# Order of the state product, the y products and level 8 in the time mixer's scan

## The chip, the cores and the metric

The kernel runs on one core of one Trainium2 chip. The metric is the device time of one execution, in microseconds. Five engines of the core matter: TensorE (PE in the profile, its weight loads listed apart as PEld), VectorE (DVE), ScalarE (ACT), GpSimd (POOL) and SyncE (SP), which here issues all transfers. Each engine works through its own list of instructions in order; the lists meet only at semaphores. Everything is fp32.

## What is computed

The model has two layers over 1024 latent tokens and 256 context tokens of width 1024. Layer 0 mixes with a grouped Fourier transform, layer 1 with a bidirectional RWKV-7 time mixer. The change is in layer 1's recurrence. For each of 16 heads, with a state s of 64 x 64, and for both directions:

```python
def step(s, inp):
    r_t, w_t, k_t, v_t, a_t, b_t = inp
    sa = einsum('bhij,bhj->bhi', s, a_t)
    s = s * w_t[:, :, None, :] + sa[..., None] * b_t[:, :, None, :] + v_t[..., None] * k_t[:, :, None, :]
    return s, einsum('bhij,bhj->bhi', s, r_t)
```

The context tokens are run first, and only their final state is used; the latent tokens start from it and give y.

## The kernel before

The work ahead of the scan (layer 0, then the features of layer 1, written to scratch in DRAM) and behind it (normalisation, gate and output projection) is not touched by the change.

The scan (function `scan`) takes two heads at a time (h = 0, 1 on partitions 0 to 63 and 64 to 127), so there are 8 outer turns j. Each goes through 10 chunks of 128 tokens, of which the first two are context and the other eight latent. A chunk is done as two sub-chunks of 64 tokens, sub 0 and sub 1, in both directions d at once. Within a sub-chunk the recurrence is put in matrix form. That needs the inverse of a triangular 64 x 64 matrix per direction and sub-chunk, which is built by doubling: levels 2, 4, 8, 16 and 32. For level k TensorE makes a first product (`t`, masked by VectorE into TT with `copy_predicated`) and a second one (`m`, copied by ScalarE to M, which VectorE then transposes to MT for the next level's second product). The last product is copied as XT.

The scan is software-pipelined over chunks. In one period (function `period`, written out by hand on each engine) the chunk c goes through its sequential part (Q_ in the code), chunk c+1 through the second stage of the inverse, levels 4 to 32 (B_), chunk c+2 through the first stage, its operand products and levels 2 and 4 (A_), and chunk c+3 gets its operands from GpSimd. There is no planner: the order on each engine is the order of the calls in its `period`.

The sequential part of a sub-chunk is a chain across engines:

- `r` (TensorE, L1779): what the state Q contributes; ScalarE copies it to R (L1558).
- `sa` (TensorE, L1789): XT times R, into bank 7; ScalarE copies it to Z in two instructions, one per head (L1563). This is "SA's copy"; the semaphore is `asa`.
- `state` (TensorE, L1799): BKt times Z, into bank 6. VectorE adds the decayed old state SP of GpSimd (L1492) and writes the new Q (L1669), for which the next `r` waits.
- for latent chunks `y_state` (TensorE, L1809) and `y` (TensorE, L1814) accumulate the outputs in bank 7; ScalarE copies them to Y (L1569), and SyncE stores them.

All level products are issued from one helper (L1729) and go by their operands. Those of the second stage share bank 5: the `m8` product (MT, TT as operands), then `t16` (M, AT), which waits for ScalarE's copy of `m8`. ScalarE's `second` is L1554. The first stage's operand products are L1722, in two groups d = 0, 1; behind the second one ScalarE copies AT (`first_at`, L1542) and VectorE writes masked parts of ar (`first_ak`, L1636); ScalarE's `first_bk` (BKt, L1546) waits for the latter. VectorE's order after `first_ak` is: state addition, the transpose MT of level 8 (L1658), `first_x` (mask MT1, then transpose M, L1629), the mask of t16 (L1615), and so on.

In the weight loads' shapes, `r`, `state` and `y` use a stationary operand of 128 rows by 64 columns, `sa`, `y_state` and all level products one of 64 x 64, and the operand products one of 64 x 128. Each fp32 matmul of the code is two instructions in the trace: a level product of 8 matmuls is listed as x16, an `r` of 4 as x8.

Of the kernel before, what the change touches and what calls it, by code (L numbers as in the profile page):

```python
# [1328 lines left out]
def count(per, j, cc, i):  # L1329

    n = PER[per]
    full, rest = divmod(cc, NCH)
    return j * sum(n) + (full * sum(n) + sum(n[:rest]) + i)
# [8 lines left out]
def scan(nc, es, sem, ps, A, fe_d, v_d, y_d, w_last):  # L1342
# [35 lines left out]
    is_lat = lambda cc: cc % NCH >= 2  # L1378
# [5 lines left out]
    def ge(eng, s, v):  # L1384

        if v > 0:
            eng.wait_ge(s, v)

    def chunk_done(eng, j, cc):

        if is_lat(cc):
            ge(eng, py, count("y", j, cc, 2))
        else:
            ge(eng, pst, count("state", j, cc, 2))

    def turn(sub, t):

        return t[:, 0:4:3] if sub == 0 else t[:, 1:3]
# [5 lines left out]
    def gcol(rows, banks, c):  # L1404

        return ps[rows, banks, :].rearrange("p e (b c t) -> p e b c t", b=2, c=4)[:, :, :, c, :]
# [21 lines left out]
    with nc.Block() as block:  # L1428
# [98 lines left out]
        @block.scalar  # L1527
        def _(act):
            act.wait_ge(msk, NMSK)

            def exps(j, cc):
                s, l = par(cc), lng(cc)
                act.wait_ge(cum_ready, count("two", j, cc, 2))
                chunk_done(act, j, cc - SETS)
                act.activation(E1[l][:, 0:264].rearrange("p (b y) -> p b y", y=66)[:, :, 1:CK + 1], cum[s][:], ACT.Exp, scale=-DECAY).then_inc(exp_ready, 1)
                ge(act, op_ready, count("operands", j, cc - 2, 2))
                act.activation(E3[s][:], cum[s][:], ACT.Exp, scale=DECAY).then_inc(exp_ready, 1)  # L1537

            def first_at(j, cc):
                act.wait_ge(pa, count("first", j, cc, PA["g1"]))  # L1540
                for h in two:
                    act.activation(d4(AT[par(cc)][own(h)]), gcol(own(h), slice(2 * h, 2 * h + 2), 3 * h), ACT.Copy).then_inc(aa, 1)  # L1542

            def first_bk(j, cc):
                act.wait_ge(da, count("dve_first", j, cc, DA["ak1"]))
                act.activation(BKt[lng(cc)][:].rearrange("p h (d b) t -> p (h d) b t", b=2), gcol(slice(0, P), slice(0, 4), 2), ACT.Copy).then_inc(aa, 1)  # L1546

            def first_m2(j, cc):
                act.wait_ge(pa, count("first", j, cc, PA["m2"]))
                act.activation(M[par(cc)][:], lev(4), ACT.Copy).then_inc(aa, 1)  # L1550

            def second(j, cc, name):
                act.wait_ge(pb, count("second", j, cc, PB["mt32" if name == "xt" else name]))
                act.activation((XT if name == "xt" else M)[par(cc)][:], lev(5), ACT.Copy).then_inc(ab, 1)  # L1554

            def r(j, c, sub):
                act.wait_ge(pr, count("two", j, c, sub + 1))
                act.activation(Rs[sub][:], seq(6), ACT.Copy).then_inc(ard, 1)  # L1558

            def sa(j, c, sub):  # L1560
                act.wait_ge(psa, count("two", j, c, sub + 1))
                for h in two:
                    act.activation(turn(sub, Z[lng(c)][own(h), h]), seq(7)[own(h)], ACT.Copy).then_inc(asa, 1)  # L1563

            def y(j, c, sub):
                if sub == 0:
                    ge(act, y_st[par(c)], j * 256 + (c - 2) // 2 * 64)
                act.wait_ge(py, count("y", j, c, sub + 1))
                act.activation(turn(sub, Y[par(c)]), seq(7), ACT.Copy).then_inc(ay, 1)  # L1569

            def period(j, c, ahead):
                A_, B_, Q_ = c + 2 >= 0 and (ahead or c + 2 < NCH), c + 1 >= 0 and (ahead or c + 1 < NCH), c >= 0
                if B_:
                    second(j, c + 1, "m4")
                if Q_:
                    r(j, c, 0)
                if ahead or c + 3 < NCH:
                    exps(j, c + 3)
                if Q_:
                    sa(j, c, 0)  # L1580
                if A_:
                    first_at(j, c + 2)
                if B_:
                    second(j, c + 1, "m8")
                if A_:
                    first_bk(j, c + 2)
                if Q_ and is_lat(c):
                    y(j, c, 0)
                if Q_:
                    r(j, c, 1)  # L1590
                    sa(j, c, 1)
                if B_:
                    second(j, c + 1, "m16")
                if Q_ and is_lat(c):
                    y(j, c, 1)
                if A_:
                    first_m2(j, c + 2)
                if B_:
                    second(j, c + 1, "xt")

            for j in range(KT):
                for c in range(0 if j else -3, NCH):
                    period(j, c, j < KT - 1)
# [104 lines left out]
        def _(pe):  # L1708
# [50 lines left out]
            def m(j, cc, k):  # L1759
                s = par(cc)  # L1760
                pe.wait_ge(db, count("dve_second", j, cc, DB[f"t{k}"]))
                level(lev(5), MT[s], TT[k][s], pb)
# [6 lines left out]
            def at(sub, d):  # L1769
                return 2 * d + (sub if d == 0 else 1 - sub)  # L1770
# [20 lines left out]

            def state(j, c, sub):
                l = lng(c)
                if not is_lat(c):
                    pe.wait_ge(asa, count("four", j, c, 2 * sub + 2))
                if c == NCH - 1 and sub == 1:
                    return
                for d, h in pairs:
                    mm = pe.matmul(seq(6)[own(h), d, :], BKt[l][:, h, at(sub, d), :], Z[l][:, h, at(sub, d), :], start=True, stop=True)  # L1799
                mm.then_inc(pst, 1)  # L1800

            def y_state(j, c, sub):
                l = lng(c)
                pe.wait_ge(asa, count("four", j, c, 2 * sub + 2))
                if sub == 0:
                    pe.wait_ge(drm, count("rmask", j, c, 1))
                for d, h in pairs:
                    o = own(h)
                    pe.matmul(seq(7)[o, d, :], ar[l][o, at(sub, d), 1, :], Q[l][o, h, at(sub, d), :], start=d == 0, stop=False, skip_group_check=True)  # L1809

            def y(j, c, sub):
                l = lng(c)
                for d, h in pairs:
                    mm = pe.matmul(seq(7)[own(h), d, :], RBK[l][:, h, at(sub, d), :], Z[l][:, h, at(sub, d), :], start=False, stop=True, skip_group_check=True)  # L1814
                mm.then_inc(py, 1)

            def period(j, c, ahead):
                A_, B_, Q_ = c + 2 >= 0 and (ahead or c + 2 < NCH), c + 1 >= 0 and (ahead or c + 1 < NCH), c >= 0
                a, b = c + 2, c + 1
                lat = Q_ and is_lat(c)  # L1820
                if Q_:
                    r(j, c, 0)
                if B_:
                    m4(j, b)
                if A_:
                    products(j, a, 0)
                if B_:
                    t(j, b, 8)
                if Q_:
                    sa(j, c, 0)  # L1830
                if A_:
                    products(j, a, 1)
                if B_:
                    m(j, b, 8)
                if lat:
                    y_state(j, c, 0)
                if Q_:
                    state(j, c, 0)
                if lat:
                    y(j, c, 0)  # L1840
                if Q_:
                    r(j, c, 1)
                if B_:
                    t(j, b, 16)
                if Q_:
                    sa(j, c, 1)
                if A_:
                    t2(j, a)
                if B_:
                    m(j, b, 16)  # L1850
                if lat:
                    y_state(j, c, 1)
                if Q_:
                    state(j, c, 1)
                if lat:
                    y(j, c, 1)
                if A_:
                    m2(j, a)
                if B_:
                    t(j, b, 32)  # L1860
                if A_:
                    t4(j, a)
                if B_:
                    mt32(j, b)

            pe.wait_ge(tab_in, 32)
            for j in range(KT):
                for c in range(0 if j else -2, NCH):
                    period(j, c, j < KT - 1)
# [61 lines left out]
```

## Time and profile before

| what | value |
|---|---|
| median of 3 runs | 2405.89 us (2400.36 to 2408.71) |
| the profiled execution | 2408.08 us |
| its span, from first to last instruction | 2406.3 us |
| TensorE matmul busy | 2179.4 us (91%) |
| TensorE weight loads | 1386.9 us (58%) |
| VectorE busy | 1123.6 us (47%) |
| ScalarE busy | 797.0 us (33%) |
| GpSimd busy | 597.9 us (25%) |
| mean granted clock | 0.971 |

The busy shares are an average over stages of different character. The scan takes about 935 us of the span, from some 1308 us on, and one period of a latent chunk in its steady part is 11.8 us long. The times of the rows below are microseconds from the start of the span. A busy TensorE is one that has a matmul in flight; since matmuls are pipelined and their ends are modelled, an order of groups is better read from the starts of their weight loads.

### The profile page before, as it was taken

The page shows a single profiled execution, that of the slowest core. Times are in us where ns is not written, and L with a number is a line of the kernel's source. Part 1 is how long each engine was busy: PE and PEld are TensorE (multiplying, and loading weights), DVE is VectorE, ACT ScalarE, POOL GpSimd, SP SyncE. Part 2 cuts the span into 40 slices and gives each one's busy share as a digit, 9 for nine tenths or more (in the row PEclk, how much of TensorE's full clock was granted, in tenths as well). Part 3 has the DMA queues.
Part 4 walks back from the last instruction along what each step waited for, and adds up shares of the span by engine and source line. Part 5 has one row for each costly group of instructions (what it writes and reads, how often), then busy time and mean ns, then how long its engine had stood idle before and what let it go on. Part 6 is the DMA issues. An engine that isn't in the chain of part 4 may idle for free. (4 is left out here: it accounts for less than half of the span.)

```text
span 2406.3 us, 55952 instructions
## 1 busy us (share of the span) xinstructions
PE 2179.4 (91%) x23884; PEld 1386.9 (58%) x23884; DVE 1123.6 (47%) x2207; ACT 797.0 (33%) x2048; POOL 597.9 (25%) x856
## 2 busy tenths in 40 slices
PE   7999999998699979999995898999989898989598
PEld 3556555354344435444443777777777777777343
DVE  4122222133846750021313666666666666666474
ACT  4111111143145522210002444444444444444332
POOL 0000000123023310000003544444445444444131
PEclk9999999999799989999997999999999999999799
DMA  8200003400137754555323343333333333332542
GB/s 348 106 26 27 27 19 127 159 36 35 38 84 197 199 161 126 155 177 175 105 79 95 86 140 100 87 87 96 86 89 87 86 87 96 84 91 66 199 140 87
DMA packets 306265, 258.49 MB, mean 107 GB/s; under 512 B 138465, under 2 KB 263649, under 8 KB 302562
## 3 DMA queue, kind: packets, MB, share of 16 engines
q1 hardware_dynamic: 306018, 254.92, 35.1%
q8 instruction: 189, 3.10, 0.5%
q14 instruction: 58, 0.48, 0.1%
HBM read 175.13 MB, written 79.69 MB: 106 GB/s over the span
## 5 line engine op out<-in xcount | busy, mean ns | idle before, releaser
L826 PE MATMUL ps<-xt,w_slab 128*128 128x512 f32 (+1 forms) x1376 | 550.2, 556 | 30.0 <-DMA w_slab<-in_w 20.0
L826 PEld LDWEIGHTS ps<-xt,w_slab 128*128 128x128 f32 x1376 | 259.8, 192 | 315.3 <-issue 262.5
L432 PE MATMUL ps<-h,fw_slab 128*128 128x512 f32 (+1 forms) x768 | 282.0, 527 | 2.1 <-ACT h L259 2.1
L1729 PE MATMUL ps<-M,AT 64*64 64x64 f32 x6400 | 270.8, 224 | 5.3 <-DVE M L1629 2.4
L1492 POOL TENSOR_TENSOR SP<-Q,decay 64x128 f32<-64x128 f32 x304 | 139.6, 459 | 464.8 <-DVE Q L1669 435.6
L1729 PEld LDWEIGHTS ps<-M,AT 64*64 64x64 f32 x6400 | 220.1, 135 | 48.8 <-issue 14.6
L1729 PE MATMUL ps<-TT,MT 64*64 64x64 f32 x5120 | 216.7, 224 | 20.3 <-ACT XT L1554 15.3
L432 PEld LDWEIGHTS ps<-h,fw_slab 128*128 128x128 f32 x768 | 145.7, 191 | 132.9 <-issue 125.4
L1729 PEld LDWEIGHTS ps<-TT,MT 64*64 64x64 f32 x5120 | 177.9, 135 | 51.4 <-issue 38.3
L1615 DVE COPY_PREDICATED TT<-mask,ps 128x256 f32<-128x256 int32 x400 | 166.8, 435 | 76.3 <-PE ps L1729 73.6
L1658 DVE STREAM_TRANSPOSE MT<-M 128x256 f32<-128x256 f32 x240 | 106.9, 446 | 148.4 <-ACT M L1554 146.0
L1722 PE MATMUL ps<-ar,bk 64*128 64x192 f32 (+1 forms) x1280 | 142.4, 342 | 24.1 <-POOL ar L1510 24.1
L588 POOL TENSOR_TENSOR xt<-scaled_out,xt 128x1024 f32<-128x1024 f32 x10 | 23.5, 2346 | 558.3 <-DVE scaled_out L621 558.3
L508 PE MATMUL ps<-h,fgo 128*128 128x512 f32 x320 | 140.8, 595 | 0.0
L1554 ACT ACTIVATE M<-ps 128x256 f32<-128x256 f32 x240 | 92.5, 385 | 121.5 <-PE ps L1729 119.6
L1505 POOL TENSOR_TENSOR bk<-feat,growth 128x256 f32<-128x256 f32 x160 | 113.3, 729 | 44.9 <-ACT growth L1537 35.3
L1722 PEld LDWEIGHTS ps<-ar,bk 64*128 64x128 f32 x1280 | 98.5, 189 | 35.7 <-issue 24.9
L1563 ACT ACTIVATE Z<-ps 64x128 f32<-64x128 f32 x320 | 87.2, 273 | 90.7 <-PE ps L1789 86.9
L1191 PE MATMUL ps<-w_last,gated 128*128 128x512 f32 x256 | 114.9, 608 | 2.2 <-DVE gated L1287 2.2
L1779 PE MATMUL ps<-Q,ar 128*64 128x64 f32 x1280 | 72.6, 235 | 47.8 <-DVE Q L1669 47.8
L1481 POOL MEMSET decay<- 128x272 f32 x5 | 1.4, 327 | 428.3 <-DMA mask_in<-in_smask 428.3
L1508 POOL TENSOR_TENSOR ar<-feat,decay 128x256 f32<-128x256 f32 x160 | 106.0, 683 | 0.0
(221 smaller groups left out, 2888.9 us busy)
## 6 DMA issues: line engine op xcount, KB each, us to landing
feat<-feature_scratch SPq DMA_DIRECT2D x160, 256.0 KB, 3.1
feature_scratch<-k_feats SPq DMA_DIRECT2D x64, 320.0 KB, 5.2
w_slab<-in_rwin SPq DMA_DIRECT2D x32, 512.0 KB, 6.2
feature_scratch<-k_feats SPq DMA_DIRECT2D x24, 640.0 KB, 6.8
mod_slab<-in_modw SPq DMA_DIRECT2D x8, 1536.0 KB, 6.5
Q<-v_token_scratch SPq DMA_DIRECT2D x320, 32.0 KB, 2.5
Z<-v_token_scratch SPq DMA_DIRECT2D x320, 32.0 KB, 2.2
fgo<-in_modw SPq DMA_DIRECT2D x8, 1024.0 KB, 8.6
```

What stands on the lines that cost most here:

```text
L432: mm = pe.matmul(ps[:, b0 + b, 0:n], wi[:, half, k, :], h0[:, k, a:a + n], start=k == 0, stop=k == KT - 1)
L508: mm = pe.matmul(ps[:, 2 * (t % 2) + b, :], fgo[:, k, cols(t)], wo[:, k, b * 512:b * 512 + 512], start=k == 0, stop=k == KT - 1)
L826: mm = pe.matmul(ps[:, bank, 0:n], w[:, i % 2, k, :], src[:, k, a:a + n], start=k == 0, stop=k == KT - 1)
L1191: mm = pe.matmul(ps[:, 2 * (n % 2) + b, :], gl[n % 2][:, k, :], wl[:, k, b * 512:b * 512 + 512], start=k == 0, stop=k == KT - 1)
L1492: g.tensor_tensor(SP[own(h)], turn(sub, Q[l][own(h), h]), pend_turn(c, own(h), sub).unsqueeze(2).broadcast_to([HD, NDIR, CK]), ALU.mult).t ...
L1505: g.tensor_tensor(d4(bk[s][:, :, slot, :]), fe(every, lo, 768), d4(E3[s][:]), ALU.mult).then_inc(op_ready, 1)
L1508: g.tensor_tensor(ar[l][:, 2 * d:2 * d + 2, 0::3, :], fe(every, 384, 256)[:, d].unsqueeze(2).broadcast_to([P, 2, 2, CK]), before(cc, every ...
L1554: act.activation((XT if name == "xt" else M)[par(cc)][:], lev(5), ACT.Copy).then_inc(ab, 1)
L1615: return v.copy_predicated(o, mask[:, m, :], i)
L1658: v.transpose(flat(MT[par(cc)][:]), flat(M[par(cc)][:])).then_inc(db, 1)
L1722: mm = pe.matmul(gp(h, d, b)[:, cols[h], :], bk[s][o, 2 * d + b, :, :], ar[l][o, 2 * d + b, cols[h], :], start=True, stop=True)
L1729: mm = pe.matmul(out[o, b, :], L[o, b, :], R[o, b, :], start=True, stop=True)
```

## The change

It moves calls in two of the hand-written orders, and puts one wait at another place.

On TensorE, the `state` product of sub-chunk 0 is issued right behind the second group of operand products, as soon as Z is there; `y_state` and `y` follow it, and `m8`, which stood ahead of all of them, comes after `y` and ahead of `r` of sub-chunk 1. Since `state` now is the first reader of Z in sub-chunk 0 of a latent chunk, it gets the wait for SA's copy; `y_state` keeps its own. On ScalarE the copy of `m8` moves behind `first_bk` and behind the copy of y of sub-chunk 0. Neither VectorE's, GpSimd's nor SyncE's order is changed, and no instruction that computes is added or removed.

```diff
@@ scalar: period
                 if A_:
                     first_at(j, c + 2)
-                if B_:
-                    second(j, c + 1, "m8")
                 if A_:
                     first_bk(j, c + 2)
                 if Q_ and is_lat(c):
                     y(j, c, 0)
+                if B_:
+                    second(j, c + 1, "m8")
                 if Q_:
                     r(j, c, 1)
                     sa(j, c, 1)
@@ tensor: state
                 l = lng(c)
-                if not is_lat(c):
+                if sub == 0 or not is_lat(c):
                     pe.wait_ge(asa, count("four", j, c, 2 * sub + 2))
@@ tensor: period
                 if A_:
                     products(j, a, 1)
-                if B_:
-                    m(j, b, 8)
-                if lat:
-                    y_state(j, c, 0)
                 if Q_:
                     state(j, c, 0)
                 if lat:
+                    y_state(j, c, 0)
                     y(j, c, 0)
+                if B_:
+                    m(j, b, 8)
                 if Q_:
                     r(j, c, 1)
```

## Rows read from the trace of the kernel before

**Rows 1.** Busy time by engine in 100 us of the scan; last: clock, DMA share, GB/s.

```profile
1500.00:1600.00 100.00, 89.95 (x2150) 76.96 (x2146) 66.81 (x175) 48.23 (x150) 49.38 (x86) 1.00 0.33 85
```

**Rows 2.** Waits from 1400 to 2200 us: total, times, longest.

```profile
PE ps L1779 <- DVE Q L1669: 40.8, 68, 0.9
DVE MT L1658 <- ACT M L1554: 122.3, 135, 1.5
```

**Rows 3.** A latent period in order of time: start, duration, engine, line, operation.

```profile
1510.13 0.63 PEld L1722 LDWEIGHTS ps<-ar,bk 64*128 64x128 f32 x8
...
1510.24 0.57 ACT L1563 ACTIVATE Z<-ps 64x128 f32<-64x128 f32 x2 [0.54 <-PE ps L1789]
1510.98 0.54 PEld L1729 LDWEIGHTS ps<-TT,MT 64*64 64x64 f32 x16 [0.23 <-issue]
...
1511.10 0.88 DVE L1636 TENSOR_TENSOR ar<-ps,scan_tab 64x256 f32<-64x256 f32 x2 [0.64 <-PE ps L1722]
...
1511.44 0.32 PEld L1809 LDWEIGHTS ps<-Q,ar 64*64 64x64 f32 x8
...
1511.82 0.31 PEld L1799 LDWEIGHTS ps<-Z,BKt 128*64 128x64 f32 x8
...
1511.90 0.39 ACT L1554 ACTIVATE M<-ps 128x256 f32<-128x256 f32 x1
1512.05 0.32 PEld L1814 LDWEIGHTS ps<-Z,RBK 128*64 128x64 f32 x8
...
1512.18 0.59 ACT L1546 ACTIVATE BKt<-ps 128x512 f32<-128x512 f32 x1
1512.39 0.61 DVE L1669 TENSOR_TENSOR Q<-ps,SP 64x128 f32<-64x128 f32 x2 [0.42 <-PE ps L1799]
1512.66 0.28 ACT L1569 ACTIVATE Y<-ps 128x128 f32<-128x128 f32 x1
1513.03 0.45 DVE L1658 STREAM_TRANSPOSE MT<-M 128x256 f32<-128x256 f32 x1
1513.06 0.31 PEld L1779 LDWEIGHTS ps<-Q,ar 128*64 128x64 f32 x8 [0.69 <-DVE Q L1669]
...
1513.44 0.54 PEld L1729 LDWEIGHTS ps<-M,AT 64*64 64x64 f32 x16
...
1513.84 0.45 DVE L1629 STREAM_TRANSPOSE M<-MT 128x256 f32<-128x256 f32 x1
...
1514.32 0.45 DVE L1615 COPY_PREDICATED TT<-mask,ps 128x256 f32<-128x256 int32 x1
```

**Rows 4.** The rest of that period, from level 16's second product on.

```profile
1514.82 0.54 PEld L1729 LDWEIGHTS ps<-TT,MT 64*64 64x64 f32 x16
...
1515.55 0.39 ACT L1554 ACTIVATE M<-ps 128x256 f32<-128x256 f32 x1 [0.58 <-PE ps L1729]
...
1515.97 0.45 DVE L1658 STREAM_TRANSPOSE MT<-M 128x256 f32<-128x256 f32 x1 [0.45 <-ACT M L1554]
...
1516.34 0.57 DVE L1669 TENSOR_TENSOR Q<-ps,SP 64x128 f32<-64x128 f32 x2
...
1516.94 0.69 DVE L1641 TENSOR_TENSOR RBK<-ps,scan_tab 128x512 f32<-128x512 f32 x1
...
1517.91 0.73 DVE L1615 COPY_PREDICATED TT<-mask,ps 128x256 f32<-128x256 int32 x2
...
1518.36 0.54 PEld L1729 LDWEIGHTS ps<-MT,TT 64*64 64x64 f32 x16 [0.37 <-DVE TT L1615]
```

**Rows 5.** The same part of a context period (no y products).

```profile
1557.05 0.55 PEld L1729 LDWEIGHTS ps<-TT,MT 64*64 64x64 f32 x16 [0.22 <-issue]
1557.66 0.31 PEld L1799 LDWEIGHTS ps<-Z,BKt 128*64 128x64 f32 x8
...
1557.17 0.88 DVE L1636 TENSOR_TENSOR ar<-ps,scan_tab 64x256 f32<-64x256 f32 x2 [0.64 <-PE ps L1722]
...
1558.87 0.45 DVE L1658 STREAM_TRANSPOSE MT<-M 128x256 f32<-128x256 f32 x1
```

## The prediction

> **What bounds the kernel now.** The change is in the scan, so I read three things of it: the busy shares of a stretch of it, the waits of TensorE and VectorE, and one period in order of time. [rows 1]: in 100 us TensorE has matmuls in flight for 89.95 us at a granted clock of 1.00, VectorE is busy 66.81, ScalarE 48.23. That looks like a TensorE bound, but one tenth is open, and [rows 2] says where: the matmul of line 1779 (call it r1, the second r of a period) waits for VectorE's new state Q, 40.8 us in 68 periods, 0.6 us each. This is the stall that the reordering reaches for. The other row of the group is the warning: VectorE waits 122.3 us for ScalarE's copies M before its transposes at line 1658. Who waits for whom does not say which wait is on the path; that takes the period.
>
> Follow [rows 3] backward from m16, the weight load of line 1729 at 1514.82. It starts 0.05 after VectorE's mask TT (1514.32 + 0.45 = 1514.77). VectorE has no gap ahead of that: the mask follows the transpose M (1513.84), that one follows the mask of MT1, that one the transpose MT of level 8 (1513.03), and this follows the state addition Q (1512.39 + 0.61 = 1513.00). From MT at 1513.03 to the mask TT at 1514.32 is 1.29 us of VectorE work back to back. Q waited for the state product st0 (1511.82, consumer 0.57 later), and that stood behind level 8's second product m8 (1510.98) and y_state (1511.44). Then [rows 4]: m16 at 1514.82, its copy M 0.73 later at 1515.55, the transpose MT at 1515.97 (0.03 after the copy's end 1515.94), Q of the second half 1516.34, RBK 1516.94, the masks TT 1517.91, whose second half releases mt32 at 1518.36. So the path is: TensorE in its order up to st0, then VectorE's queue from Q on, to the end of the period. The transpose MT of level 8 is a link of it: whatever starts it later lengthens the period, and an earlier r1 by itself shortens nothing.
>
> **The change part by part.** I move the orders to their new places and take times of [rows 3]. All before product group 1 (line 1722, at 1510.13) is untouched, so TensorE is free at 1510.98 as now.
>
> State product first. It now has to wait for ScalarE's copy Z: the row starts at 1510.24 and lasts 0.57, so it ends at 1510.81, before 1510.98. The new wait is free; behind it in TensorE's queue stand y_state, y, m8 and r1. Its cover is 0.17 us; if Z came later, all of them would move by the excess. y_state's own wait is for the same count and adds nothing. st0 starts at 1510.98 instead of 1511.82.
>
> TensorE groups of another shape. Between groups of one shape, 8 matmuls take 0.23 (st0 1511.82 to y 1512.05) and 16 take 0.46 (m8 1510.98 to y_state 1511.44). Where the stationary operand's rows change between 64 and 128, 8 take 0.38, in both directions: y_state 1511.44 to st0 1511.82, and r1 1513.06 to t16 1513.44. That is 0.15 per change. The old order from group 1 on was m8 and y_state (64), st0, y and r1 (128), t16 (64): changes at st0 and t16. The new one is st0 (128), y_state (64), y (128), m8 (64), r1 (128), t16 (64): after group 1 five changes between row counts instead of two. Group 1 itself (64 rows by 128 columns) has a change behind it either way, and I take its slot as it is, 0.85. It has no row with a 128-row group behind it: as a ready change it may be already in the 0.85 (0 more), or cost a further 0.15 as the others; I take 0, since m8 behind it already was of another tile width (its loads take 0.63 and then none is issued for the rest of the slot), and keep 0.15 for the range. So st0 1510.98, y_state 1511.36, y 1511.74, m8 1512.12, r1 not before 1512.12 + 0.46 + 0.15 = 1512.73. m8 starts 1.14 us later than now.
>
> The Trainium skill, page "TensorEngine Tiling (Array Packing)", section Key Properties, says that changing the tiling mode, not just the tile, drains TensorE. By that rule interleaving 64-row and 128-row groups is what an order should avoid, and it speaks against this change; the rows' 0.15 agrees with it. Without the rule one would put 0.23 for each of the three moved groups of 8, and m8 at 1511.67; that case is a rival below.
>
> VectorE's Q. st0 would allow 1510.98 + 0.57 = 1511.55, but the additions to ar at 1511.10 last until 1511.98 and stand ahead of it in the queue. So Q runs 1511.98 to 1512.59 instead of 1512.39 to 1513.00: 0.41 earlier. r1 could start at 1512.65 and goes at 1512.73, 0.33 earlier than now. This stall is indeed gone.
>
> ScalarE's order. Before, it copied level 8's M at 1511.90, then BKt 1512.18, then Y 1512.66. Now BKt is first; it needs ar, which ends at 1511.98, so with the 0.06 from VectorE's end to another engine (Q's end 1513.00 to r1 1513.06) it starts at 1512.04. BKt to Y was 0.48 from start to start, so Y starts at 1512.52 (its product, at most 0.61 after y, is there at 1512.35), and Y leaves ScalarE free some 0.2 to 0.3 later, at 1512.7 to 1512.8. The M copy waits for m8: 1512.12 + 0.73 = 1512.85. It ends at 1513.24. So in a latent period the product decides and not the place behind Y.
>
> What is late next. The transpose MT starts at 1513.24 + 0.03 = 1513.27; now it is 1513.03. VectorE, which has Q done at 1512.59, sits idle for 0.68 us in between, because transpose, masks and M stand in order behind MT. t16 needs the copy too, starts at 1513.29 (now 1513.44) and stalls 0.18 for it; its product is there at 1514.02, before VectorE comes to its mask at 1513.27 + 1.29 = 1514.56. m16 then starts at 1514.56 + 0.50 = 1515.06 against 1514.82. Everything behind it in [rows 4] hangs on it. The cost is 0.24 us in a latent period. GpSimd's SP gets Q sooner, which helps nobody: no wait in the chain is for SP.
>
> Context periods (no y, no y_state), [rows 5]. Now: m8 1557.05, st0 1557.66 (0.61 for 16 with a change), ar 1557.17 to 1558.05, MT 1558.87. New: st0 1557.05, m8 1557.43, product at 1558.16. But ScalarE now must do BKt first, and that waits for ar: 1558.11, M at 1558.59 (0.48 on), end 1558.98, MT 1559.01. Here the queue order costs, 0.14 us. Q would have let MT go at about 1558.7.
>
> **The sum.** The scan has 8 pairs of heads times 10 chunks: 64 latent and 16 context periods. The last two periods of all have less in them (no work for later chunks); I put these two at nothing, as one may gain what the other loses. 62 x 0.24 = 14.9 and 16 x 0.14 = 2.2, together 17.1 us. The profiled execution took 2408.08 us (span 2406.3 and 1.8 around it), so it would be 2425.2; the median shown is 2405.89, lower by 2.2, so the forecast is 2405.9 + 17.1 = 2423.0 us. The work before and behind the scan is the same.
>
> **The rivals.**
> A. The changes of shape don't cost (they overlap, as the groups are queued up and ready). m8 starts at 1510.98 + 3 x 0.23 = 1511.67, its product is there at 1512.40, ScalarE comes to it only behind Y, at about 1512.72, and MT starts at 1513.14: 0.11 late. 62 x 0.11 + 2.2 = 9 us, 2415. For it: no row has these very neighbours. Against: both directions of [rows 3] show 0.38.
> B. Group 1 to st0 costs 0.15 more, with a further change or the added wait: 0.39 a period, 62 x 0.39 + 2.2 = 26.4 us, 2432. For it: the pair of neighbours is new. Against: the 0.85 slot seems to hold a change.
> C. The other side: faster, because Q and r1 decide. If the MT of level 8 could follow Q, it would start at 1512.62, 0.41 earlier, and r1 by TensorE's order 0.33 earlier; then the period shortens by 0.33, 62 x 0.33 = 20 us, 2385. The point: m8's copy must end by 1512.59, so m8 must start by 1511.47, while three groups of 8 stand ahead of it, which take 0.69 even at 0.23 each (1511.67). For it: r1's wait of 40.8 us is TensorE's largest. Against: that arithmetic, and VectorE's unbroken row from MT to TT.
> D. Nothing: MT is late but m16 is not, since something not in the rows absorbs 0.24. There is only the 0.05 between TT's end and m16, so it is unlikely. 2406.
>
> **How the numbers follow.** Forecast 0.60, A 0.13, B 0.09, C 0.10, D 0.08. A measurement of this kernel tells about 0.3%, 7 us, from no change. Slower by more than that: forecast, A and B, 0.82; I move 0.01 of it to the same side, since A is near the bound: slower 0.81, same 0.09, faster 0.10. The range is 2409 to 2433: it holds the forecast, A and B and leaves out C and D.
>
> **What would show it.** In the profile after: the waits list r1 for Q only shortly or not at all, and new rows of t16 for ScalarE's M (about 0.2 us each) and of line 1658 for M rise by some 0.7 us a period. From group 1 to m8's first load is 1.14 us in a latent period, 0.38 in a context one. Q starts as ar ends. The period is 0.24 longer from r to r. It is wrong if m16 starts earlier than 4.69 us after group 1 (now 1510.13 to 1514.82), or if the changes of shape are not seen at the three new places.

## The result, and the profile after

| kernel | median | ratio to before (95% interval) | span of the profiled execution |
|---|---|---|---|
| before | 2406.12 us (2400.36 to 2408.71, 4 runs) | | 2406.3 us |
| changed | 2457.32 us (2453.09 to 2459.49, 4 runs) | 1.0214 (1.019 to 1.0238) | 2457.2 us |

The change costs 51.2 us. The forecast was a loss of 17.1 and a range that ended at 2433: the direction was right, the size three times too small.

The weight loads of r (line 1779) give the period. In a latent one from sub 0's r to the next sub 0's it was 11.80 us (1507.17 to 1518.97); it is now 12.60 (1505.82 to 1518.42). In context periods it went from 11.56 (1553.25 to 1564.81) to 11.73 (1567.47 to 1579.20).

The waits of the changed kernel from 1400 to 2200 us (engine, line, released by: total, times, longest), some of them:

```profile
DVE MT L1658 <- ACT M L1554: 170.4, 194, 1.5
...
PEld ps L1729 <- DVE M L1629: 59.4, 65, 1.1
...
PE ps L1729 <- DVE M L1629: 50.5, 65, 0.9
...
PE ps L1779 <- DVE Q L1669: 6.6, 13, 0.5
```

The stall of r1 for Q, 40.8 us in [rows 2], is down to 6.6. The wait of MT for M has grown from 122.3 to 170.4. And a wait that [rows 2] had no room for has come: TensorE now stands for VectorE's M (line 1629), 0.8 us in each of 65 periods.

The same stretch of a latent period as [rows 3] (start, duration, engine, line, operation):

```profile
1508.77 0.63 PEld L1722 LDWEIGHTS ps<-ar,bk 64*128 64x128 f32 x8
...
1509.62 0.31 PEld L1799 LDWEIGHTS ps<-Z,BKt 128*64 128x64 f32 x8 [0.23 <-ACT Z L1563]
...
1510.01 0.31 PEld L1809 LDWEIGHTS ps<-Q,ar 64*64 64x64 f32 x8
1510.38 0.31 PEld L1814 LDWEIGHTS ps<-Z,RBK 128*64 128x64 f32 x8
...
1510.54 0.60 DVE L1669 TENSOR_TENSOR Q<-ps,SP 64x128 f32<-64x128 f32 x2
...
1510.77 0.54 PEld L1729 LDWEIGHTS ps<-TT,MT 64*64 64x64 f32 x16
...
1511.22 0.88 POOL L1492 TENSOR_TENSOR SP<-Q,decay 64x128 f32<-64x128 f32 x2 [6.51 <-DVE Q L1669]
1511.38 0.31 PEld L1779 LDWEIGHTS ps<-Q,ar 128*64 128x64 f32 x8
...
1511.50 0.38 ACT L1554 ACTIVATE M<-ps 128x256 f32<-128x256 f32 x1
...
1511.91 0.45 DVE L1658 STREAM_TRANSPOSE MT<-M 128x256 f32<-128x256 f32 x1 [0.77 <-ACT M L1554]
...
1512.23 1.59 POOL L1505 TENSOR_TENSOR bk<-feat,growth 128x256 f32<-128x256 f32 x2
1512.28 0.98 DVE L1615 COPY_PREDICATED MT<-mask,AT 128x256 f32<-128x256 int32 x1
...
1513.29 0.45 DVE L1629 STREAM_TRANSPOSE M<-MT 128x256 f32<-128x256 f32 x1
1513.77 0.45 DVE L1615 COPY_PREDICATED TT<-mask,ps 128x256 f32<-128x256 int32 x1
...
1514.27 0.54 PEld L1729 LDWEIGHTS ps<-TT,MT 64*64 64x64 f32 x16
```

Read it against [rows 3] from group 1 (1508.77 here, 1510.13 there). m8 starts 2.00 after it, and started 0.85 after it; MT comes at 3.14 instead of 2.90, 0.24 late. Then look at the line that the prediction took for granted, the mask of MT1 at 1512.28: 0.98 us, where it took 0.41. It is not listed as waiting. It is listed as long. The GpSimd row above it, bk, starts 0.05 earlier and takes 1.59 for two instructions. In the kernel before, GpSimd's rows of this stretch were these, on either side of the mask at 1513.40:

```profile
1513.08 0.97 POOL L1492 TENSOR_TENSOR SP<-Q,decay 64x128 f32<-64x128 f32 x2 [5.73 <-DVE Q L1669]
1513.40 0.41 DVE L1615 COPY_PREDICATED MT<-mask,AT 128x256 f32<-128x256 int32 x1
...
1514.18 1.42 POOL L1505 TENSOR_TENSOR bk<-feat,growth 128x256 f32<-128x256 f32 x2
```

bk came 0.37 us after the mask was done. From MT to the mask TT it is now 1.86 us instead of 1.29. m16 (1514.27) stands 5.50 after group 1 instead of 4.69, 0.81 later, and 0.80 is what the period grew by.

The same in sums over the scan, 1308 to 2300 us (times in us and mean ns of one), first before, then changed:

```profile
L1615 DVE COPY_PREDICATED MT<-mask,AT 128x256 f32<-128x256 int32 x79 | 32.2, 408 | 0.0
```

```profile
L1615 DVE COPY_PREDICATED TT<-mask,ps 128x256 f32<-128x256 int32 x398 | 165.9, 435 | 73.6 <-PE ps L1729 70.8
...
L1615 DVE COPY_PREDICATED MT<-mask,AT 128x256 f32<-128x256 int32 x79 | 64.6, 818 | 0.0
```

The 398 masks whose data come from PSUM kept their 435 ns. Only the 79 whose data (AT) lie in SBUF beside the mask became long. It is not the operation as such that suffers: in [rows 3] the mask TT at 1514.32, with its data in PSUM, ran wholly beside bk (1514.18) and took 0.45.

### The profile page after: what moved, and what is told of

It reads as the page before. It is cut to its first block and busy times, and to the rows that moved or that the text cites. A ratio compares the mean times of both kernels' runs of the same rounds, so it can differ in the third digit from the quotient of the medians.

```text
span 2457.2 us, 55952 instructions
## 1 busy us (share of the span) xinstructions
PE 2201.2 (90%) x23884; PEld 1398.3 (57%) x23884; DVE 1140.2 (46%) x2207; ACT 802.0 (33%) x2048; POOL 591.0 (24%) x856
## 5 line engine op out<-in xcount | busy, mean ns | idle before, releaser
L1492 POOL TENSOR_TENSOR SP<-Q,decay 64x128 f32<-64x128 f32 x304 | 121.7, 400 | 518.5 <-DVE Q L1669 474.8
L1505 POOL TENSOR_TENSOR bk<-feat,growth 128x256 f32<-128x256 f32 x160 | 123.1, 791 | 48.2 <-ACT growth L1537 38.7
L508 PEld LDWEIGHTS ps<-h,fgo 128*128 128x128 f32 x320 | 59.6, 190 | 76.3 <-issue 76.3
```

The costliest lines, as they stand in the source:

```text
L508: mm = pe.matmul(ps[:, 2 * (t % 2) + b, :], fgo[:, k, cols(t)], wo[:, k, b * 512:b * 512 + 512], start=k == 0, stop=k == KT - 1)
L1492: g.tensor_tensor(SP[own(h)], turn(sub, Q[l][own(h), h]), pend_turn(c, own(h), sub).unsqueeze(2).broadcast_to([HD, NDIR, CK]), ALU.mult).t ...
L1505: g.tensor_tensor(d4(bk[s][:, :, slot, :]), fe(every, lo, 768), d4(E3[s][:]), ALU.mult).then_inc(op_ready, 1)
```

## The experiments

Theory 1: VectorE's mask of MT1 reads two operands from SBUF and is held while a GpSimd instruction that reads SBUF runs. The change brought them together from both sides: Q is earlier, so GpSimd's SP and then bk are, and MT is later, so the mask is. Theory 2: the mask is slow from something else at its new place, and GpSimd has no part in it.

**e1, bk after the mask.** In GpSimd's `operands(j, cc)` of the changed kernel:

```diff
                 ge(g, pa, count("first", j, cc - 2, PA["g1"]))
+                if cc - 1 >= 0:
+                    g.wait_ge(da, count("dve_first", j, cc - 1, DA["mt1"]))
```

> The changed kernel, but GpSimd starts the operands (bk, ar) of a chunk only after VectorE's mask of MT1 in the same period is done. Theory 1 (the mask, which reads two operands from SBUF, is held while GpSimd's bk runs): the mask takes 0.41 instead of 0.98 us, level 8's MT to the mask TT takes 1.29 again, a latent period 12.04 instead of 12.60; 56 x 0.57 and 8 x 0.27, 34 us less than the changed kernel, about 2423. Theory 2 (the mask is slow from something else at its new place, ScalarE's copies or TensorE's reads of AT; GpSimd doesn't matter): the mask stays at 0.98 and the time at 2457. Theory 3 (GpSimd's own delay then becomes the bound): mask 0.41, but the operand products wait for ar, above 2423.

Measured 2425.02 us, ratio 1.007 (1.0053 to 1.0087). One period of it (VectorE and GpSimd):

```profile
1505.84 0.45 DVE L1660 STREAM_TRANSPOSE MT<-M 128x256 f32<-128x256 f32 x1 [0.77 <-ACT M L1556]
...
1506.20 0.41 DVE L1617 COPY_PREDICATED MT<-mask,AT 128x256 f32<-128x256 int32 x1
1506.64 0.45 DVE L1631 STREAM_TRANSPOSE M<-MT 128x256 f32<-128x256 f32 x1
1506.78 1.41 POOL L1507 TENSOR_TENSOR bk<-feat,growth 128x256 f32<-128x256 f32 x2 [0.77 <-DVE MT L1617]
```

One more wait, on an engine that is idle most of the time, takes 32 us off. The mask is at 0.41, bk at 1.41, and MT still waits 0.77 for M. What is left over the kernel before is the loss that was forecast, 17 to 19 us. Theory 2 falls.

**e2, TensorE's order only.** The changed kernel with ScalarE's old order:

```diff
+                if B_:
+                    second(j, c + 1, "m8")
                 if A_:
                     first_bk(j, c + 2)
                 if Q_ and is_lat(c):
                     y(j, c, 0)
-                if B_:
-                    second(j, c + 1, "m8")
```

> TensorE's new order with the new wait, ScalarE's order as before (M of level 8 ahead of BKt and Y). Theory 1: in a latent period the copy waits for m8's product either way, so MT and the collision stay where they are; only the context periods give back 0.14 each, 2 us: 2455. Rival: ScalarE's queue is what made MT late, and with its old order most of the loss is gone: 2425 or less.

Measured 2449.65 us, ratio 1.0173 (1.0158 to 1.0188). Latent periods are as in the changed kernel (1501.37 to 1513.96, 12.59 us): the product of m8 decides there, not the place of its copy. Context periods are 11.28 us (1563.00 to 1574.29), 0.45 less than in the changed kernel: 16 of them are 7.2 of the 7.7 us by which the two differ. Of the 0.45, MT is 0.38 (2.40 after group 1 instead of 2.78) and a mask of 0.41 instead of 0.47 the rest. So ScalarE's move costs more in context periods than the 0.14 I gave it: with TensorE's order alone they are 0.28 shorter than in the kernel before.

**e3, ScalarE's order only.** The ScalarE part of the change, in the kernel before.

> ScalarE's new order alone, TensorE's order as before. M of level 8 is copied behind BKt and Y, at about 2.71 us after group 1 instead of 1.77, so MT is 0.23 late while Q, SP and bk stay. Theory 1: the mask then falls on GpSimd's second SP instruction and is held for 0.1 to 0.4 more: 62 x (0.33 to 0.63) + 2, so 2428 to 2447. Theory 2: 62 x 0.23 + 2, 2422, with a mask of 0.41.

Measured 2422.26 us, ratio 1.0056 (1.0041 to 1.0071). One period of it:

```profile
1517.50 1.14 POOL L1492 TENSOR_TENSOR SP<-Q,decay 64x128 f32<-64x128 f32 x2 [5.73 <-DVE Q L1669]
1517.62 0.45 DVE L1658 STREAM_TRANSPOSE MT<-M 128x256 f32<-128x256 f32 x1 [0.20 <-ACT M L1554]
...
1517.98 0.41 DVE L1615 COPY_PREDICATED MT<-mask,AT 128x256 f32<-128x256 int32 x1
```

MT is 0.18 late (3.08 after group 1, at 1514.54), and the mask takes 0.41, which is the number I had given to theory 2. But see the row above: the pair of SP instructions takes 1.14 here, 0.97 in the kernel before and 0.88 in the changed one. The second of the pair, listed by itself, starts at 1517.97, takes 0.67 instead of 0.40 and ends 0.24 after the mask: here GpSimd was held, and the mask was not. My expectation had the collision and gave it to the wrong side. In the last latent period of each turn the same run has it the other way, with a mask of 0.83 behind a GpSimd instruction that began 0.15 before it:

```profile
1552.93 0.68 POOL L1513 TENSOR_TENSOR ar<-feat,decay 128x256 f32<-128x256 f32 x1
1553.08 0.83 DVE L1615 COPY_PREDICATED MT<-mask,AT 128x256 f32<-128x256 int32 x1
```

**e5 and e8, bk onto the mask.** The kernel before, all orders but GpSimd's untouched:

```diff
                 if j or cc >= 3:
-                    g.wait_ge(sp_ready, count("scaled", j, cc - 3, 4 if cc % NCH != 2 else 2))
+                    g.wait_ge(sp_ready, count("scaled", j, cc - 3, 2))
+                    g.wait_ge(dst, count("four", j, cc - 3, 2))        # e5; in e8: ... + 2
...
                 (the two bk instructions)
+                if (j or cc >= 3) and (cc - 3) % NCH < NCH - 1:
+                    g.wait_ge(op_ready, count("operands", j, cc, 2))
+                    state_scaled(j, cc - 3, 1)
+                    g.wait_ge(sp_ready, count("scaled", j, cc - 3, 4))
```

> The kernel before, its orders on TensorE, ScalarE and VectorE untouched; on GpSimd bk waits for Q of sub 0 and goes ahead of SP of sub 1, so bk starts at Q's end, 0.3 us ahead of the mask of MT1. Theory 1 (the mask is held until the bk instruction that runs is done): bk's first ends 0.70 after Q, the mask ends 0.34 after that, so it shows 0.72 instead of 0.41; 0.31 in each of some 78 periods, 24 us: 2431. Theory 2 (GpSimd doesn't matter): mask 0.41, 2407.

e5 measured 2409.24 us, ratio 1.0005 (0.9996 to 1.0014), and tests nothing of this: the count waited for was of the state before, so bk ran 3 us too early. It does show that the added waits and the new order on GpSimd cost next to nothing by themselves (its mask takes 0.45, beside SP). (Not shown above: at its old place SP of sub 1 is left out.)

> As e5, but with the wait for the state that sub 0 of this period writes (e5's count was that of the state before it, so bk ran 3 us too early and the mask met only the end of an SP instruction). Now bk starts at Q's end, about 0.3 us ahead of the mask. Theory 1: the mask shows about 0.72 instead of 0.41 in each of some 78 periods, 24 us more than before: 2431. Theory 2: mask 0.41, no more than the kernel before, 2407.

e8 measured 2440.03 us, ratio 1.0142 (1.0125 to 1.0159). One period of e8:

```profile
1517.15 0.45 DVE L1663 STREAM_TRANSPOSE MT<-M 128x256 f32<-128x256 f32 x1
1517.35 1.59 POOL L1506 TENSOR_TENSOR bk<-feat,growth 128x256 f32<-128x256 f32 x2 [6.25 <-DVE Q L1674]
1517.52 0.86 DVE L1620 COPY_PREDICATED MT<-mask,AT 128x256 f32<-128x256 int32 x1
1518.41 0.45 DVE L1634 STREAM_TRANSPOSE M<-MT 128x256 f32<-128x256 f32 x1
```

The loss comes without any of the change, from GpSimd's order alone: the mask takes 0.86 and the period 12.25 us (1504.92 to 1517.17), 0.45 more. It is more than my 0.31 because bk starts 0.23 after Q and not at once. bk's first instruction, listed by itself, takes 0.73, so it runs until 1518.08, and the mask ends at 1518.38, 0.30 after it. In the changed kernel the same sum gives 1512.23 + 0.73 + 0.30 = 1513.26, and the mask ends at 1513.26. So it is throughout: wherever the mask is held, by bk in 53 masks of the changed kernel and 76 of e8, it ends 0.30 to 0.31 after the end of that first instruction, whether bk began 0.05 or 0.17 ahead of it. This is the mechanism with its number.

**e6, an instruction with one operand in SBUF.** In the changed kernel:

```diff
-                masked(flat(MT1[s][:]), flat(AT[s][:]), 0).then_inc(da, 1)
+                v.transpose(flat(MT1[s][:]), maskf[:, 0, :]).then_inc(da, 1)
```

> The changed kernel with the mask of MT1 replaced by a transpose of a constant table into MT1, so this instruction reads one operand from SBUF and not two (the masking of level 1 is left out). It starts beside bk as before. Theory 1, narrow (only a VectorE instruction with two operands in SBUF is held): 0.45 us, the time falls to about 2427. Theory 1, broad (every VectorE instruction out of SBUF is held while bk runs): 0.9 to 1.0, and 2457.

Measured 2425.09 us, ratio 1.0064 (1.0047 to 1.0081). One period of it:

```profile
1504.25 1.42 POOL L1505 TENSOR_TENSOR bk<-feat,growth 128x256 f32<-128x256 f32 x2
1504.30 0.40 DVE L1627 STREAM_TRANSPOSE MT<-mask_in 128x256 f32<-128x256 f32 x1
```

bk starts 0.05 ahead of VectorE's instruction, as in the changed kernel, and neither holds the other. The operation is another one here too, but the mask TT with its data in PSUM, at 0.45 beside bk, has only the mask in SBUF and is the same operation. The narrow form stands: what is held is the instruction with two operands in SBUF. The time is that of e1 from the other side.

**e4, the state product first and nothing else moved.** In the kernel before, with the new wait in `state`:

```diff
-                if B_:
-                    m(j, b, 8)
-                if lat:
-                    y_state(j, c, 0)
                 if Q_:
                     state(j, c, 0)
+                if B_:
+                    m(j, b, 8)
                 if lat:
+                    y_state(j, c, 0)
                     y(j, c, 0)
```

> TensorE: state product first, then m8, then y_state and y; ScalarE's order as before. m8 is 0.38 later than in the kernel before and its copy ends at 2.35 us after group 1, ahead of Q's end at 2.46, so MT follows Q at once, 0.41 earlier than before, and GpSimd's SP and bk move with Q, so that they stand to the mask as before. My theory: 62 x 0.41 + 16 x 0.19, 28 us less than before: 2378, mask 0.41. Rival: r1 or something behind it becomes the bound and little is gained: 2400 to 2406. Second rival: the mask meets bk here too, and 0.57 a period more makes it slower than before: 2413.

Measured 2376.09 us, ratio 0.9867 (0.9853 to 0.9882): 31 us faster than before, the best of the study, and 81 us ahead of the changed kernel, which differs in where m8 and its copy stand. One period of it:

```profile
1507.67 0.63 PEld L1722 LDWEIGHTS ps<-ar,bk 64*128 64x128 f32 x8
...
1508.52 0.31 PEld L1799 LDWEIGHTS ps<-Z,BKt 128*64 128x64 f32 x8 [0.22 <-ACT Z L1563]
...
1508.90 0.54 PEld L1729 LDWEIGHTS ps<-TT,MT 64*64 64x64 f32 x16
...
1509.44 0.60 DVE L1669 TENSOR_TENSOR Q<-ps,SP 64x128 f32<-64x128 f32 x2
...
1510.07 0.45 DVE L1658 STREAM_TRANSPOSE MT<-M 128x256 f32<-128x256 f32 x1
...
1510.12 0.97 POOL L1492 TENSOR_TENSOR SP<-Q,decay 64x128 f32<-64x128 f32 x2 [5.22 <-DVE Q L1669]
...
1510.44 0.41 DVE L1615 COPY_PREDICATED MT<-mask,AT 128x256 f32<-128x256 int32 x1
```

m8 is only 0.38 behind the state product, so its copy is done before Q, and MT follows Q without a gap at 2.40 us after group 1 (2.90 before). bk moves with Q and stays as far behind the mask as it was (0.77 behind its start, 0.78 before). Only in the last latent period of each turn does the mask fall on one of GpSimd's ar instructions, and take 0.80.

**e7, e4 with ScalarE's new order.**

> TensorE's order of e4 (state, m8, y_state, y), with ScalarE's new order. m8 is early, but its copy stands behind Y, whose product comes at 2.57 us after group 1; the copy ends at 3.16, MT at 3.19 instead of 2.40, and bk, which follows the early Q, falls on the mask again. Theory 1: period about 12.6, 2455 to 2460, mask 0.98. If the place of m8 in TensorE's order were what costs, it would be near e4's 2376.

Measured 2455.77 us, ratio 1.0192 (1.0177 to 1.0207). MT is 2.25 behind the start of ar (1508.46 to 1510.71), which is 0.97 behind group 1: 3.22, forecast 3.19. The mask takes 0.89:

```profile
1510.71 0.45 DVE L1658 STREAM_TRANSPOSE MT<-M 128x256 f32<-128x256 f32 x1 [0.85 <-ACT M L1554]
...
1510.95 1.59 POOL L1505 TENSOR_TENSOR bk<-feat,growth 128x256 f32<-128x256 f32 x2
1511.08 0.89 DVE L1615 COPY_PREDICATED MT<-mask,AT 128x256 f32<-128x256 int32 x1
```

So each half of the change that delays the M of level 8 is enough alone, once the state product is early: m8 behind y (e2, 2450) or the copy behind Y (e7, 2456).

## Why the prediction was right in direction and wrong in size

- **The path.** That MT of level 8 is a link and r1's stall is not was right. e1 and e6 have next to no stall of r1 and are slower than before; e3 keeps the stall (40.3 us) and is slower by about as much; the changed kernel has lost the stall and is slower than all three.
- **TensorE's order.** Right. The slots in the changed kernel are 0.39, 0.37, 0.39 and 0.61 (1509.62 to 1511.38), forecast 0.38, 0.38, 0.38 and 0.61. Group 1's slot stayed 0.85 with a 128-row group behind it, so rival B is out, and the new wait shows no cost. Rival A is out as well: the changes of shape do cost, 0.15 each.
- **MT's delay.** Right: 3.14 us after group 1, as forecast, 0.24 late. In context periods MT was 0.11 late (2.78 for 2.67), forecast 0.14; the mask, which begins 0.23 after the second SP and takes 0.47, adds 0.06 that was not in the sum, and the period grew by 0.17.
- **What is late next: this step failed.** The prediction carried "1.29 us of VectorE work back to back" from [rows 3] to the new place as a constant, and said that GpSimd gets Q sooner, "which helps nobody". It hurt. SP starts 0.69 ahead of MT now (1511.22, 1511.91), and started 0.05 behind it in the old order (1513.08, 1513.03). So bk, which began 0.78 behind the mask, begins 0.05 ahead of it, and the mask is held: 0.57 us in a latent period. 0.24 + 0.57 is the 0.81 by which m16 is late. With e1, which takes just this hold away, the forecast sum comes out: 2425.02 us, against 2423.0 forecast. Part of that is luck: a steady latent period of e1 grew by 0.22 for 0.24 (12.02), the last two latent ones of a turn by 0.32 (11.74 for 11.42, 11.37 for 11.05), which the sum had not told apart, and the context ones by 0.17 for 0.14.
- **The sum.** Six periods of a turn grew by 0.80, the seventh latent one by 0.80 too (12.22 for 11.42), the last by 0.59 (11.64 for 11.05; there the mask meets GpSimd's last operands and takes 0.68), the two context ones by 0.17: 6.5 us a turn, 8 turns, 52. The last two periods of all grew by 0.2 each, and in two others (masks at 1672.68 and 1905.78) the mask was not held, since bk came late or was the one that waited; 51.2 was measured.
- **Rival C** named the right point, m8's copy done before Q. Three groups of 8 ahead of m8 are too many, one is not: e4 collects the prize. Its size was put too low: 0.33 us a period and 20 in all, where e4 has 0.51 (11.29 for 11.80) and 31. MT comes 0.50 earlier there and not 0.41, as Q starts at 1.77 after group 1, where the sums had it at 1.85, behind the end of ar.
- **The signs of being wrong.** Both that the prediction named at its end stayed quiet: m16 did not come early (5.50 after group 1), and the changes of shape were seen. None asked for the length of the mask. What did fail is the period from r to r, 0.80 longer for 0.24. And the sign "from group 1 to m8's first load is 1.14 us" is not what its own sums say: 1.14 is how much later m8 starts, at 1.99 after group 1, and it came at 2.00.

The Trainium skill has the rule that I passed over: page "SBUF — State Buffer", section "SBUF: two separate sides", says that VectorE and GpSimd share one pair of SBUF ports under an exclusive lock, that a VectorE instruction with two SBUF inputs takes part (against a GpSimd one that reads SBUF), and that whoever starts first keeps the pair for the whole instruction. By this rule and the order of the rows it is told at once which of the masks is at risk. The runs agree on the hold, on its length and on who takes part: the mask ends 0.30 after bk's first instruction (changed kernel, e8), GpSimd waits in its turn (the second SP of e3), and an instruction with one SBUF operand is free (e6). They show that one holds the other; that the cause is a pair of ports is the page's word. Who was first can't be read off rows that start less than 0.05 us apart: in e3 the second SP starts 0.02 ahead of the mask and is the one that waits, while bk at 0.05 ahead in the changed kernel makes the mask wait. At 1905.75 there, 0.03 ahead, bk waits: its first instruction takes 0.99 and the mask 0.41.

## What to carry to other kernels

When an engine off the path gets its input earlier, follow it through its queue and lay its instructions over those of the engine that shares a resource with it; a duration from a trace holds only with the same neighbours. A held instruction is listed as long and not as waiting, so after a change of order compare mean durations by form before looking for new waits. Split a change that moves several calls: here one of them alone is worth 31 us, and the others turned it into a loss of 51.

## What the runs showed of the hardware

- A `COPY_PREDICATED` of 128 x 256 with mask and data in SBUF took 0.41 us alone and 0.86 to 0.98 when a GpSimd `TENSOR_TENSOR` of 128 x 256 (0.73 us) had begun 0.05 to 0.17 us before it, the longer the nearer (changed kernel, e8); with data in PSUM it took 0.435 on average in all of these kernels.
- A GpSimd `TENSOR_TENSOR` of 64 x 128 took 0.67 instead of 0.40 us when it met that mask and the mask was not held (e3).
- On TensorE a change between 64 and 128 stationary rows from one group to the next cost 0.15 us: 0.37 to 0.39 from start to start instead of 0.23 for 8 matmuls, 0.61 instead of 0.46 for 16. It did in both directions, and also where the change recurs at each of four neighbouring groups.
